# Seven block products instead of eight in the first feed-forward, activation sums on VectorE

## The reference

```python
def swiglu(x, w_gate, w_up, w_down):
    return (jax.nn.silu(x @ w_gate) * (x @ w_up)) @ w_down

h = x + 0.5 * rmsnorm(swiglu(rmsnorm(x, g1), w1_gate, w1_up, w1_down), g1_post)
h = h +       rmsnorm(mixer(rmsnorm(h, g_mix), ...), g_mix_post)
h = h + 0.5 * rmsnorm(swiglu(rmsnorm(h, g2), w2_gate, w2_up, w2_down), g2_post)
```

## Time and profile before

| | |
|---|---|
| median of 3 runs | 1116.28 us |
| profiled execution | 1118.97 us |
| its span | 1117.2 us |
| TensorE busy | 1096.3 us (98%) |
| weight loads busy | 944.4 us (85%) |
| VectorE busy | 576.8 us (52%) |
| ScalarE busy | 455.4 us (41%) |
| GpSimd busy | 55.3 us (5%) |
| mean granted clock of TensorE | 0.998 |

### The profile page before, as it was taken

How to read it: one execution, slowest core, us unless ns; L and a number is a source line. 1 busy time by engine, 2 the same in 40 slices (tenths; PEclk the granted TensorE clock), 3 DMA queues, 4 the chain that set the end, 5 groups by cost and what they waited for, 6 DMA issues and landing times.

```text
span 1117.2 us, 14939 instructions
## 1 busy us (share of the span) xinstructions
PE 1096.3 (98%) x5910; PEld 944.4 (85%) x5910; DVE 576.8 (52%) x703; ACT 455.4 (41%) x661; POOL 55.3 (5%) x83
## 2 busy tenths in 40 slices
PE   7999999999999999998999999999999999999998
PEld 5888888888888888887878888889899999998886
DVE  5434443443333754456565333446788778763334
ACT  6222222232223474666765222325454454442222
POOL 2000000000000200000000000004600000000001
PEclk9999999999999999999999999999999999999999
DMA  9532333323322345222114335224423424233311
GB/s 299 152 104 85 112 94 94 94 94 104 102 95 60 106 141 151 76 76 58 38 39 127 98 96 169 94 76 161 160 76 99 129 76 140 87 132 133 98 52 76
DMA packets 133331, 118.81 MB, mean 106 GB/s; under 512 B 6416, under 2 KB 119072, under 8 KB 133280
## 3 DMA queue, kind: packets, MB, share of 16 engines
q1 hardware_dynamic: 131104, 113.38, 33.1%
q10 hardware_dynamic: 1456, 2.10, 0.9%
q0 software_dynamic: 720, 2.62, 0.6%
HBM read 109.70 MB, written 6.29 MB: 104 GB/s over the span
## 4 chain that ended last, share of the span: by engine, by line
PE 88%; DVE 5%; ACT 4%; issue 2%; DMA 1%; POOL 0%; SPq 0%; ACTq 0%; DVEq 0%; POOLq 0%
PE bank L1405 24%; PE bank L1395 12%; PE bank L1396 12%; PE bank L1397 12%; PE bank L1525 5%; PE bank L1524 5%; PE bank L1523 5%; PE bank L1637 1%; PE bank L1638 1%; PE bank L1639 1%; DVE w_lo L917 1%; PE bank L1460 1%; PE bank L1461 1%; PE bank L1462 1%; DMA raw<-in_ffn_w_up 1%
## 5 line engine op out<-in xcount | busy, mean ns | idle before, releaser
L917 DVE TENSOR_TENSOR w_lo<-raw,w_hi 128x1024 fp32r<-128x1024 f32 x130 | 166.1, 1279 | 213.2 <-ACT w_hi L503 213.1
L1395 PE MATMUL bank<-u_hi,w_hi 128*128 128x512 f32 x600 | 236.2, 394 | 0.2 <-issue 0.2
L1397 PE MATMUL bank<-u_hi,w_lo 128*128 128x512 f32 x600 | 233.8, 390 | 0.0
L1396 PE MATMUL bank<-u_lo,w_hi 128*128 128x512 f32 x600 | 233.7, 390 | 0.0
L503 ACT ACTIVATE w_hi<-raw 128x1024 fp32r<-128x1024 f32 x130 | 137.1, 1055 | 186.5 <-PE bank L1405 86.1
L1397 PEld LDWEIGHTS bank<-u_hi,w_lo 128*128 128x128 f32 x600 | 112.7, 188 | 24.0
L1395 PEld LDWEIGHTS bank<-u_hi,w_hi 128*128 128x128 f32 x600 | 112.8, 188 | 23.1 <-issue 0.5
L1396 PEld LDWEIGHTS bank<-u_lo,w_hi 128*128 128x128 f32 x600 | 112.9, 188 | 22.4 <-issue 0.2
L1405 PE MATMUL bank<-w_hi,a_hi 128*128 128x512 f32 x408 | 126.0, 390 | 0.0
L1405 PE MATMUL bank<-w_lo,a_hi 128*128 128x512 f32 x408 | 125.7, 389 | 0.0
L1405 PE MATMUL bank<-w_hi,a_lo 128*128 128x512 f32 x408 | 125.7, 389 | 0.0
(11 more groups left out here) (240 smaller groups left out, 1674.2 us busy)
## 6 DMA issues: line engine op xcount, KB each, us to landing
raw<-in_ffn_w_down SPq DMA_DIRECT2D x40, 512.0 KB, 3.4
raw<-in_w_in SPq DMA_DIRECT2D x40, 512.0 KB, 3.8
raw<-in_ffn_w_up SPq DMA_DIRECT2D x26, 512.0 KB, 3.9
raw<-in_ffn_w_gate SPq DMA_DIRECT2D x25, 512.0 KB, 3.8
raw<-in_ffn_w_gate SPq DMA_DIRECT2D x5, 1024.0 KB, 5.3
raw<-in_ffn_w_up SPq DMA_DIRECT2D x5, 1024.0 KB, 8.1
h_store<-h SPq DMA_DIRECT2D x2, 2048.0 KB, 9.9
h<-h_store SPq DMA_DIRECT2D x2, 2048.0 KB, 9.5
```

What stands on the lines that cost most here:

```text
L917: V.tensor_tensor(w_lo[:, slot(u), :], raw[:, slot(u), :], w_hi[:, slot(u), :].bitcast(F32), ALU.subtract).then_inc(lo_ready, 1)
L1395: mm(dst, w_hi[:, slot(u), w], rhs_hi[:, k - k0, :], start=k == k0, stop=False)
L1396: mm(dst, w_hi[:, slot(u), w], rhs_lo[:, k - k0, :], start=False, stop=False)
L1397: last = mm(dst, w_lo[:, slot(u), w], rhs_hi[:, k - k0, :], start=False, stop=k == k1)
```

## The change

- The first feed-forward uses the code of the second for both layers (`ffn(u0, layer)`): two pairs as before, nine pairs as seven products of half blocks. Its loops are written out. Layer-dependent counts go into every wait.
- In the first layer VectorE multiplies the three gate pieces of a pair by rstd ahead of silu (`quad_scale`). The second multiplication by rstd is left out: all hidden values of a token then carry the same factor 1/rstd, which the norm behind the down projection takes out again. Its eps is scaled for that (`eps_pre`): 4 x 1e-6 x (mean square + 1e-6).
- x is in h only for its squares, since h takes the weights of every second pair; x is loaded a second time during the down projection (`x_back`). The gain vectors of the boundary are loaded later.
- The eight activation sums of each layer are done by VectorE and not by GpSimd: in the first layer four of them among the rstd instructions at the start and four among the first units, in the second layer ahead of and among the first units.
- `rstd_all` moves to another place, and the down projection of the first layer takes its token tiles in the order 0, 1, 3, 2.

```diff
-FFN_UNITS = 2 * KF + KF
+CLASSIC = 2
+QP = KF // 2 - CLASSIC
+STEPS = 7
+FFN_UNITS = 4 * CLASSIC + STEPS * QP + KF
...
# SP
+                for q in range(QP):
+                    if q == 0:
+                        sp.wait_ge(lo_ready, U_STR[layer])
+                    elif q > 1:
+                        sp.wait_ge(lo_ready, str_unit(layer, q - 2, STEPS))
+                    elif layer:
+                        sp.wait_ge(h_kept, 32)
+                    else:
+                        sp.wait_ge(pre_ms, TT)
+                    cols = slice((q + CLASSIC) * 2 * P, (q + CLASSIC + 1) * 2 * P)
+                    for m, w in enumerate((wg, wu)):
+                        sp.dma_start(pair_raw[q % 2][:, m, :, :], kmajor(w, cols)).then_inc(pair_in[q % 2], 16)
+                for n in range(KF):
...
+                    elif n == 2 * SLOTS:
+                        for t in range(TT):
+                            sp.dma_start(h[:, t, :], x[t * P:(t + 1) * P, :]).then_inc(x_back[t], 16)
...
# VectorE
+            def quad_scale(q, n):
+                done = 3 * q
+                tile, r = ((both[:, 0, 0, 0:TOK], rstd_all[:, 0:TOK]), (both[:, 0, 1, :], rstd_all),
+                           (both[:, 0, 0, TOK:N], rstd_all[:, TOK:N]))[n]
+                src = tile
+                if n < 2:
+                    dve.wait_ge(quad_ready, done + (1, 3)[n])
+                else:
+                    src = bank[:, BY[q % 2][0], 0:TOK]
+                    dve.wait_ge(unit_used, str_unit(0, q, STEPS))
...
+                V.tensor_tensor(tile, src, r, ALU.mult).then_inc(quad_scaled, 1)
...
+            def token_whole(layer, m):
+                kh, th = ((0, 1), (1, 1), (0, 0), (1, 0))[m]
...
+                V.tensor_tensor(quarter(u_sum, kh, th), quarter(u_hi, kh, th).bitcast(F32),
+                                quarter(u_lo, kh, th).bitcast(F32), ALU.add).then_inc(u_whole, 1)
...
+            def token_sum(layer, m):
...
+                V.tensor_tensor(t_sum[:, t, :, :], x, y, ALU.subtract).then_inc(t_whole, 1)
...
                     for n in range(STEPS):
                         if n == 0 and q:
-                            pair_lo(q, 3)
-                            pair_sum_of(q, "S4")
-                            quad_mul(q - 1, 0)
-                            quad_mul(q - 1, 1)
+                            if layer == 0:
+                                quad_scale(q - 1, 2)
+                            pair_lo(layer, q, 3)
+                            pair_sum_of(layer, q, "S4")
+                            quad_mul(layer, q - 1, 0)
+                            quad_mul(layer, q - 1, 1)
...
                         if n >= 4:
-                            quads(q, n - 4)
+                            quads(layer, q, n - 4)
+                            if layer == 0 and n != 5:
+                                quad_scale(q, n // 6)
...
                 dve.wait_ge(pre_rstd, t + 1)
                 V.tensor_scalar(rstd_diag[:, t * P:(t + 1) * P], ident[:, :], rstd_pre[:, t:t + 1], None,
                                 ALU.mult).then_inc(diag_ready, 1)
+                token_whole(0, t)
             split(3)
...
# GpSimd
+                if n < TT:
+                    pool.wait_ge(eps_set, 1)
+                    G.tensor_tensor(ve_post[:, c], ms_post[:, c], eps_pre[:, c], ALU.add).then_inc(post_ve, 1)
...
+            pool.wait_ge(t_whole, 4)
             G.dma_start(g_post, gain(g1post)).then_inc(g_post_in, 16)
+            pool.wait_ge(quad_hidden, 3 * QP)
             G.dma_start(g_pre, gain(gmpre)).then_inc(g_pre_in, 16)
```

More of the change, by code:

```diff
@@ L452, in _ @@
                     load(U_OUT + k, w_out[k * P:(k + 1) * P, :])
[L453 to L475, removed]
+            ffn_loads(1, U_FFN2, w2g, w2u, w2d, 0)
             for t in range(TT - 1):
@@ L1120, in ffn2, with ffn @@
+            def ffn(u0, layer):
+                if layer:
+                    for m in range(4):
+                        token_whole(layer, m)
                 for j in range(4 * CLASSIC):
                     i, jj = j // 4, j % 4
+                    if layer == 0 and j == 0:
+                        split(u0 + 4)
+                        split(u0 + 5)
+                        dve.wait_ge(rstd_kept, 1)
+                    if jj % 2 == 0 and layer == 0:
+                        dve.wait_ge(unit_used, u0 + j + 1)
+                        if i:
+                            dve.wait_ge(hidden_ready, PAIRS + j // 2 - 1)
+                        V.tensor_tensor(silu[:, jj // 2, :], bank[:, jj, :], rstd_all, ALU.mult).then_inc(z_scaled, 1)
@@ L1475, in first_units, with moving, product @@
                     part(j, 2, 4, True)
-            def ffn(u0, layer, a0, b):
+            def moving(n, part, k):
+                if n in (0, 3, 6):
+                    kh, th = {0: (0, 0), 3: (1, 0), 6: (1, 1)}[n]
+                    return (u_hi, u_lo)[part][:, kh * KD // 2 + k, th * TOK:(th + 1) * TOK]
+                return tc[:, {1: T_3, 2: T_2, 4: T_1, 5: T_4}[n], part, k, :]
+            def product(layer, q, n, m):
+                u = str_unit(layer, q, n)
+                b = (BY[q % 2], BW, BY[q % 2], BX, BY[q % 2], BW, BY[q % 2])[n][m]
+                dst, first = bank[:, b, 0:TOK], n in (0, 1, 3)
+                for k in range(KD // 2):
+                    w = slice((m * KD // 2 + k) * P, (m * KD // 2 + k + 1) * P)
+                    mm(dst, w_hi[:, slot(u), w], moving(n, 0, k), start=first and k == 0, stop=False, skip_group_check=True)
+                    mm(dst, w_hi[:, slot(u), w], moving(n, 1, k), start=False, stop=False, skip_group_check=True)
+                    last = mm(dst, w_lo[:, slot(u), w], moving(n, 0, k), start=False, stop=k == KD // 2 - 1, skip_group_check=True)
+                return last
@@ L1478, in ffn @@
+            def ffn(u0, layer):
                 if layer:
[L1479 removed]
+                    first_units(2, u0)
                 else:
                     earliest_units()
[L1482 to L1487 removed]
@@ L1492, in down @@
                     pe.wait_ge(a_lo_ready, i * 4 + (a0 + k + 1))
-                    for n, t in enumerate((0, 2, 3, 1)):
-                        if first and t < 2:
-                            pe.wait_ge(hidden_ready, PAIRS + layer * KF + KF - 1 + t)
+                    for t in (0, 1, 3, 2):
+                        if first and t == 2:
+                            pe.wait_ge(quad_hidden, 3 * (layer + 1) * QP)
+                        elif first and t == 3:
+                            pe.wait_ge(quad_ready, 3 * (layer + 1) * QP)
                         last = token_product(ud + k, t, first, False)
```

508 lines of the change are left out of this document (210 added, 298 removed).

## The result

The changed kernel takes 1104.06 us (median of 4 runs, 1103.49 to 1105.26) against 1116.32 us for the kernel before (median of 4, 1115.69 to 1116.60). The ratio is 0.9883 with a 95% interval of 0.987 to 0.9896: 12.3 us less, where 14.0 were forecast (1102.3). Two later series of the changed kernel gave ratios of 0.9876 (0.9856 to 0.9896) and 0.9897 (0.9877 to 0.9916). The difference depends on the series: 12.3 us in the first, 14.0 and 11.0 in the two later ones (1118.61 to 1104.57, 1116.52 to 1105.56). Over all runs on record, the kernel before has 28 between 1115.46 and 1119.71 with a median of 1116.67, the changed one 12 between 1102.91 and 1105.72 with a median of 1104.58: 12.1 us by the medians, 12.9 by the means (1117.42 and 1104.49).

A forecast was written before the change was run, and what follows sets the result against it. The first feed-forward was taken as bound by the number and pace of TensorE's matmuls. -14.4 us for matmuls + 0.4 for VectorE's tight spot = -14.0, from 1116.28 to 1102.3 us; range 1101.2 to 1105.3.

The forecast's parts named there:

- Matmuls: First layer's gate and up products: nine pairs of seven products replace 36 classic units, 14.4 us off TensorE's stream.
- Tight spot: Seventh unit of each first-layer pair waits for VectorE's second quads: margin 0.31 us, charged 0.4 us in nine pairs.
- First pair: Loads of pair 0 in the first layer arrive before TensorE's first unit needs them: cost 0, up to 3 us once.
- Start, down projection, boundary: First layer's start, its down projection and the boundary behind it: cost 0, up to 0.3 us for GpSimd's eps addition.
- Second layer: Activation sums moved from GpSimd to VectorE in the second layer: TensorE waits for none of it, gain 0.
- A: The forecast case: TensorE sets the pace of the first layer's pairs, 1101.5 to 1103.2 us; chance 0.74.
- C: First layer's first pair late, its loads sharing DMA engines with pair 1 and g_post: 1103.3 to 1105.3 us; chance 0.05.
- B: Quads late for the seventh unit in each first-layer pair, eating part of the gain: 1103.2 to 1106.5 us; chance 0.14.

The follow-up runs named there:

- e1: Changed kernel with VectorE's scaling of unit 6's gate result moved ahead of the hidden product of units 4 and 5; 1103.67 us (0.9875).
- e8: Changed kernel with unit 6's gate scaling moved early and the gain vector g_post loaded only behind the last pair; 1103.16 us (0.986).
- e2: Changed kernel with two more VectorE multiplications of 256 columns, output unused, behind quad_scale(0) in every first-layer pair; 1109.38 us (0.9928).
- e0: The changed kernel run once more with no edit, as base for the others; 1104.57 us (0.9876).
- e9: The changed kernel run again with no edit, to compare its start with the kernel before; 1105.56 us (0.9897).
- e3: Changed kernel with the second layer's eight activation sums back on GpSimd; 1103.62 us (0.9868).
- e4: Changed kernel with SP issuing the loads of pair 1 only when pair 0 has landed; 1104.48 us (0.9883).
- e6: Changed kernel with only the load of the gain vector g_post moved behind the last pair; 1102.82 us (0.9871).
- e7: Changed kernel with the first layer's eight activation sums on GpSimd, ahead of the load of g_post; 1108.27 us (0.991).

## Why the prediction was right, and which step failed

- **Matmuls, right.** 195.84 us of classic units against 181.43 for the nine pairs in e1 and e8. The 120 ns a matmul from the second layer held. The 21 us that the prediction worked out by the Trainium skill's formula ("TensorE: Matmul & The Clock Gate", Back-to-back issue gap) were not there. That section gives the formula for a lone matmul and says that in a stream with a weight load per matmul it comes out too long at 512 columns; here it is too short, 215.8 ns against 226.7.
- **Tight spot, mechanism right, charge wrong.** 0.31 us of margin was worked out, 0.38 measured (93.54 to 93.92), since the scaling delays the second quads by 0.46 us and not by 0.53. The 0.4 us charged for nine pairs were 0: none of the eight later pairs waits. e2 shows that the margin was just what it seemed.
- **First pair, wrong.** The step that failed is "Cost 0, up to 3 us once": it cost 2.0 us in the first trace, 1.0 and 1.8 in e0 and e9. I had given 9.6 us of lead and called it ample since the second layer does with 7.3, or 8.5 with the two multiplications. In all seven traces of this order with a wait there (after, e0, e3, e4, e6, e7, e9) the excess of the first pair plus the lead is 9.28 to 9.30 us, for example 22.17 - 20.16 + (54.47 - 47.20) = 9.28 and 20.84 - 20.16 + (54.66 - 46.04) = 9.30. So the need is 9.3 us, and the lead was 7.27. Instead of 1.1 us to spare 2.0 were missing, and the 3.1 us between them are three terms. The need was 0.8 us larger: the order adds a wait of 1.65 us on ScalarE, which I had not followed (e1; without it the need is some 7.6, an estimate). The load took 9.75 us and not 8.4, 1.3 more, through g_post (e6), which I had named and put at nothing. And the loads were issued 17.0 us ahead of the stage and not 18.0: I took the start from one trace, a late one, and with an early start the low part of unit 7, for which they wait, is not early by as much (17.0 to 17.2 us ahead with starts up to 54.7, 18.2 in e0 and e1 with starts at 56.3 and 56.0). The need alone would have fitted into the 9.6 us.
- **Start, down projection, boundary, right.** Unit 3's low part is in time; from the down projection's first matmul to the first transposes 111.55 us against 111.53 before. GpSimd's four additions with two operands take 0.19 to 0.59 us, the seven with one operand 0.22 to 0.59.
- **Second layer, right**, and shown by e3.
- **The sum.** Stage 183.45 instead of 195.84: 12.4 us less by the first trace, 13.4 by e0. Of the 14.4 us of the matmuls, 1 to 2 went into the first pair, and the 0.4 charged for the tight spot did not fall due. The measured time, 1104.06, lies above what I gave for A (1101.5 to 1103.2, chance 0.74) and in what I gave for C (1103.3 to 1105.3, chance 0.05): C's late first pair happened beside A's even pace, through g_post as C says but not through pair 1, and through the order on VectorE, which C does not name. It showed as C's single wait, yet at the place of B's, ahead of the seventh unit. That the profiled time came out at the forecast 1105 is luck: the start was 2.6 us earlier and the mixer 1.3 longer than in the trace before. What is left between the series (11.0 to 14.0 us) fits the scatter of the clock at the start and in the mixer; no run separates the two. An early start makes the kernel before shorter in full, the changed one only in part: the stage of the trace after starts 1.84 us ahead of e0's and ends 0.85 ahead.

What stays open: whether the longer stretch at half clock in the mixer is more frequent with the change. It was 6.8 us in five of the ten traces of the changed kernel and its variants, and in none of the four of the kernel before; it costs 1.0 to 1.6 us more than the one of 3.4, and wasn't separated from chance.

## What to carry to other kernels

Where a stage is copied to another place, its steady state can be read off the copy to the hundredth, but its first round cannot: there it meets other queues, other transfers and another lead. Follow each in-order queue there for a round trip (here scale, silu, high part, low part) and move the first step of the trip ahead of work that no one waits for. And take a lead over an engine from several traces, since the starts of single ones lie 2.1 us apart (55.05 to 57.11 in the kernel before).

## What the runs showed of the hardware that was not expected

- 0.5 MB from GpSimd's queue, issued 1.4 us behind a 2 MB transfer of SP's queue, costs it 1.3 us (8.41 us in e6 against 9.75); issued 5.0 us behind it, nothing that shows (8.45 in e7). Of 2 MB behind it in SP's own queue no effect shows (9.58 in e4 without them, 9.56 to 9.97 with them).
- A matmul in these streams has a fixed cost of some 13 ns beside its columns: 120.0 ns with 256 columns and 226.7 with 512 make 2 x 120.0 - 226.7 = 13.3.
- A wait of TensorE that shows as 0.18 us costs 0.44 (e2): 0.16 lie under the busy time of the matmul ahead, and the matmul behind the one that waited comes 0.10 us late again.
- A wait of 2.12 us on TensorE at 35 us was followed by 3.4 us at half clock (e7), while 1.29 us at 73 us was not.
